# The first token tile multiplied with two weight chunks before the second tile is loaded and transposed

## The reference

```python
h = rmsnorm(x, g_mix[l])        # x: (1, 256, 1024) float32
proj = h @ w_in[l]              # w_in: (1024, 4608) float32
...
x = x + merged @ w_out[l]
h = rmsnorm(x, g_ffn[l])
x = x + jnp.square(jax.nn.relu(h @ w_ff1[l])) @ w_ff2[l]
return rmsnorm(x, g_final)
```

## Time and profile before

| what | value |
|---|---|
| median of three runs | 355.31 us (355.11 to 355.83) |
| the profiled execution, its own time | 355.15 us |
| span of its trace | 353.3 us |
| TensorE busy | 346.1 us (98%) |
| VectorE busy | 253.6 us (72%) |
| ScalarE busy | 186.8 us (53%) |
| DMA | 64.24 MB, mean 182 GB/s |

### The profile page before, as it was taken

How to read it: one execution, slowest core, us unless ns; L and a number is a source line. 1 busy time by engine, 2 the same in 40 slices (tenths; PEclk the granted TensorE clock), 3 DMA queues, 4 the chain that set the end, 5 groups by cost and what they waited for, 6 DMA issues and landing times.

```text
span 353.3 us, 4554 instructions
## 1 busy us (share of the span) xinstructions
PE 346.1 (98%) x1717; PEld 285.6 (81%) x1717; DVE 253.6 (72%) x309; ACT 186.8 (53%) x227; POOL 4.0 (1%) x14
## 2 busy tenths in 40 slices
PE   8999999999999999999999999999999999999993
PEld 4788888777778888888888888888888888888882
DVE  2969999999899889956756737638376383663734
ACT  4995644688885457443654436424364253542413
POOL 1000000000000000000000000000000000000000
PEclk9999999999999999999999999999999999999999
DMA  7999456444533366683637571935719447160003
GB/s 271 353 386 380 169 177 196 160 124 163 181 131 119 121 237 189 231 280 107 206 120 239 181 253 51 334 133 166 255 56 318 155 153 255 67 237 0 0 0 120
DMA packets 34286, 64.24 MB, mean 182 GB/s; under 512 B 1344, under 2 KB 5600, under 8 KB 34272
## 3 DMA queue, kind: packets, MB, share of 16 engines
q1 hardware_dynamic: 33968, 63.52, 53.3%
q10 hardware_dynamic: 304, 0.53, 0.4%
HBM read 63.00 MB, written 1.05 MB: 181 GB/s over the span
## 4 chain that ended last, share of the span: by engine, by line
PE 94%; issue 2%; DMA 1%; SPq 1%; DVE 1%; ACT 1%; POOLq 0%; POOL 0%; DVEq 0%
PE ps L885 20%; PE ps L887 20%; PE ps L886 20%; PE ps L1115 17%; PE ps L1117 9%; PE ps L872 3%; PE ps L931 2%; PE ps L942 1%; DMA raw<-in_w_in_dram 1%; PE ps L985 1%; PE ps L1010 1%; SPq L310 0%; DVE w_lo L630 0%; SPq L314 0%; DVE res L852 0%
## 5 line engine op out<-in xcount | busy, mean ns | idle before, releaser
L885 PE MATMUL ps<-w_hi,a_lo 128*128 128x512 f32 x272 | 107.5, 395 | 0.0
L887 PE MATMUL ps<-w_lo,a_hi 128*128 128x512 f32 x272 | 106.1, 390 | 0.0
L886 PE MATMUL ps<-w_hi,a_hi 128*128 128x512 f32 x272 | 106.0, 390 | 0.0
L1115 PE MATMUL ps<-b_both,w_hi 128*128 128x512 f32 x256 | 90.8, 399 | 0.0
L1117 PE MATMUL ps<-b_both,w_lo 128*128 128x256 f32 x256 | 71.9, 281 | 0.0
L836 DVE TENSOR_TENSOR w_lo<-raw,w_hi 128x2048 fp32r<-128x2048 f32 x28 | 63.5, 2288 | 6.4 <-ACT w_hi L596 6.4
L392 ACT CAST w_hi<-raw 128x2048 fp32r<-128x2048 f32 (+1 forms) x30 | 53.7, 1796 | 18.0 <-PE ps L887 16.8
L622 DVE TENSOR_TENSOR w_lo<-raw,w_hi 128x2048 fp32r<-128x2048 f32 x26 | 59.4, 2288 | 3.4 <-ACT w_hi L392 3.3
L885 PEld LDWEIGHTS ps<-w_hi,a_lo 128*128 128x128 f32 x272 | 51.1, 188 | 11.1 <-issue 0.7
L887 PEld LDWEIGHTS ps<-w_lo,a_hi 128*128 128x128 f32 x272 | 51.0, 188 | 11.0
L886 PEld LDWEIGHTS ps<-w_hi,a_hi 128*128 128x128 f32 x272 | 51.1, 188 | 10.1
(11 more groups left out here) (116 smaller groups left out, 245.1 us busy)
## 6 DMA issues: line engine op xcount, KB each, us to landing
raw<-in_w_ff_dram SPq DMA_DIRECT2D x32, 1024.0 KB, 5.5
raw<-in_w_in_dram SPq DMA_DIRECT2D x14, 1024.0 KB, 5.9
raw<-in_w_out_dram SPq DMA_DIRECT2D x4, 1024.0 KB, 4.9
raw<-in_w_in_dram SPq DMA_DIRECT2D x14, 256.0 KB, 5.1
raw<-in_w_attn_up_dram SPq DMA_DIRECT2D x2, 1024.0 KB, 5.0
raw<-in_w_conv_pw_dram SPq DMA_DIRECT2D x2, 1024.0 KB, 5.0
res<-in_x_dram SPq DMA_DIRECT2D x2, 512.0 KB, 3.9
raw<-in_w_in_dram SPq DMA_DIRECT2D x4, 128.0 KB, 3.9
```

Of the source, the lines that this page charges most:

```text
L885: nc.tensor.matmul(dst, lo[:, tok], w_hi[:, slot, k], start=start, stop=False, skip_group_check=seeded)
L886: nc.tensor.matmul(dst, hi[:, tok], w_hi[:, slot, k], start=False, stop=False, skip_group_check=seeded)
L887: return nc.tensor.matmul(dst, hi[:, tok], w_lo[:, slot, k], start=False, stop=stop, skip_group_check=seeded)
L1115: nc.tensor.matmul(ps[:, TB + c], w_hi[:, slot, k, cols], b_both[:, kk].rearrange("p a t -> p (a t)"), start=kk == 0, stop=False)
```

## The change

x tile 1 is loaded behind chunks 0 and 1 of the weights. PE transposes tile 0 and goes on to the products of tile 0 with chunks 0 and 1; only then does it transpose tile 1, and the products of tile 1 with the two chunks follow. ACT and DVE make `a_hi` and `a_lo` of chunks 0 and 1 for each tile apart (128x128), and DVE makes `w_lo` of chunks 0 and 1 in two instructions of 128x512. The matmuls on zeros ahead of the products go from three to one. The number of matmuls that count, and everything from chunk 2 on, stay as they were.

```diff
-WARM_AGAIN = 3
+WARM_AGAIN = 1
...
-            for t in range(TT):
-                sp.dma_start(res[:, t], x_v[:, t]).then_inc(x_full[t], 16)
+            sp.dma_start(res[:, 0], x_v[:, 0]).then_inc(x_full[0], 16)
             for k in range(2):
                 load_halves(0, slice(k, k + 1), first_full[k])
+            sp.dma_start(res[:, 1], x_v[:, 1]).then_inc(x_full[1], 16)
...
+            act.wait_ge(x0_tr, 1)
+            for k in range(2):
+                nc.scalar.activation(a_hi[:, k, 0:P], x_chunk(k)[:, 0:P], ACT.Copy, scale=gmix[:, k:k + 1]).then_inc(x0_hi, 1)
+            act.wait_ge(first_full[1], 32)
+            nc.scalar.copy(w_hi[:, 0, 1], raw[:, 0, 1]).then_inc(first_hi[1], 1)
             for pair in range(4):
                 act.wait_ge(x_tr, pair + 1)
+                tok = slice(P, T) if pair == 0 else slice(0, T)
                 for k in (2 * pair, 2 * pair + 1):
-                    nc.scalar.activation(a_hi[:, k], x_chunk(k), ACT.Copy, scale=gmix[:, k:k + 1]).then_inc(xt_hi, 1)
-                if pair == 0:
-                    act.wait_ge(first_full[1], 32)
-                    nc.scalar.copy(w_hi[:, 0, 1], raw[:, 0, 1]).then_inc(first_hi[1], 1)
+                    nc.scalar.activation(a_hi[:, k, tok], x_chunk(k)[:, tok], ACT.Copy, scale=gmix[:, k:k + 1]).then_inc(xt_hi, 1)
...
+            for k in range(2):
+                dve.wait_ge(x0_hi, k + 1)
+                input_low(k, slice(0, P), x0_lo)
+            for k in range(2):
+                dve.wait_ge(first_hi[k], 1)
+                nc.vector.tensor_tensor(w_lo[:, 0, k], raw[:, 0, k], w_hi[:, 0, k].bitcast(F32),
+                                        ALU.subtract).then_inc(first_lo, 1)
...
+            for k in range(2):
+                pe.wait_ge(x0_hi, k + 1)
+                pe.wait_ge(first_hi[k], 1)
+                chunk_product(0, k, a_hi, w_hi, start=k == 0)
+                pe.wait_ge(x0_lo, k + 1)
+                chunk_product(0, k, a_lo, w_hi)
+            pe.wait_ge(first_lo, 1)
+            chunk_product(0, 0, a_hi, w_lo)
+            pe.wait_ge(x_full[1], 16)
+            for k in range(KD):
+                last = transpose(x_chunk(k)[:, P:T], res[:, 1, k * P:k * P + P])
+                if k % 2 == 1:
+                    last.then_inc(x_tr, 1)
+            pe.wait_ge(first_lo, 2)
+            chunk_product(0, 1, a_hi, w_lo)
+            for k in range(2):
                 pe.wait_ge(xt_hi, k + 1)
-                pe.wait_ge(first_hi[k], 1)
-                half_products(0, k, a_hi, start=k == 0)
+                chunk_product(1, k, a_hi, w_hi, start=k == 0)
+                chunk_product(1, k, a_hi, w_lo)
+            for k in range(2):
                 pe.wait_ge(xt_lo, k + 1)
-                half_products(0, k, a_lo)
+                chunk_product(1, k, a_lo, w_hi)
```

More of the change, by code:

```diff
@@ L227, in build @@
         vec_made = sem("vec_made")
+        x0_tr = sem("x0_tr")
+        x0_hi = sem("x0_hi")
+        x0_lo = sem("x0_lo")
         x_tr = sem("x_tr")
@@ L635, in _, with input_low @@
             dve.wait_ge(gmix_made, 1)
+            def input_low(k, tok, made):
+                nc.vector.scalar_tensor_tensor(out=a_lo[:, k, tok], in0=x_chunk(k)[:, tok], scalar=gmix[:, k:k + 1],
+                                               in1=a_hi[:, k, tok].bitcast(F32), op0=ALU.mult,
+                                               op1=ALU.subtract).then_inc(made, 1)
+            for k in range(2):
[5 more added lines that the diff above has]
+                                        ALU.subtract).then_inc(first_lo, 1)
             for pair in range(4):
@@ L638, in _ @@
                     dve.wait_ge(xt_hi, k + 1 if pair == 0 else 2 * pair + 2)
[L639 to L645, removed]
+                    input_low(k, slice(P, T) if pair == 0 else slice(0, T), xt_lo)
                 if pair == 1:
@@ L916, in _ @@
             transpose(ps[:, SB0, 0:KD], gmix_rows).then_inc(gmix_tr, 1)
[L917 to L922, removed]
+            pe.wait_ge(x_full[0], 16)
+            for k in range(KD):
+                last = transpose(x_chunk(k)[:, 0:P], res[:, 0, k * P:k * P + P])
+                if k == 1:
+                    last.then_inc(x0_tr, 1)
             for _ in range(WARM_AGAIN):
                 nc.tensor.matmul(ps[:, 0], zero_b[:, 0:P], zero_b[:], start=True, stop=True)
-            def half_products(n, k, a, start=False):
-                for t in range(TT):
-                    nc.tensor.matmul(ps[:, t], a[:, HK * n + k, t * P:t * P + P], w_hi[:, n, k], start=start, stop=False)
             def high_products(n, k):
-                half_products(n, k, a_lo)
-                half_products(n, k, a_hi)
+                for a in (a_lo, a_hi):
+                    for t in range(TT):
+                        nc.tensor.matmul(ps[:, t], a[:, HK * n + k, t * P:t * P + P], w_hi[:, n, k], start=False, stop=False)
             def low_products(n, k):
@@ L944, in low_products, with chunk_product @@
                 return last
-            for k in (0, 1):
+            def chunk_product(t, k, a, w, start=False):
+                nc.tensor.matmul(ps[:, t], a[:, k, t * P:t * P + P], w[:, 0, k], start=start, stop=False)
+            for k in range(2):
[7 more added lines that the diff above has]
+            pe.wait_ge(x_full[1], 16)
+            for k in range(KD):
+                last = transpose(x_chunk(k)[:, P:T], res[:, 1, k * P:k * P + P])
[4 more added lines that the diff above has]
+            for k in range(2):
                 pe.wait_ge(xt_hi, k + 1)
-                pe.wait_ge(first_hi[k], 1)
-                half_products(0, k, a_hi, start=k == 0)
+                chunk_product(1, k, a_hi, w_hi, start=k == 0)
+                chunk_product(1, k, a_hi, w_lo)
+            for k in range(2):
                 pe.wait_ge(xt_lo, k + 1)
-                half_products(0, k, a_lo)
-            pe.wait_ge(first_lo, 1)
-            for k in (0, 1):
-                low_products(0, k)
+                chunk_product(1, k, a_lo, w_hi)
             pe.wait_ge(xt_lo, 4)
```

## The result

The changed kernel takes 356.23 us (median of 10 runs, 355.66 to 356.69) against 355.24 (10 runs, 355.02 to 355.83): a ratio of 1.0024, 95% interval 1.0017 to 1.0032. It is slower by 0.99 us in the medians, just beyond the 0.2% (0.7 us) up to which I had called a change told from none. The profiled execution has 356.50 us and a span of 354.7, for 355.15 and 353.3 before.

What follows compares the result with a forecast made beforehand. TensorE bounds the kernel, so the head counts only through the start of chunk 2's first product. ScalarE's later `high(0)` moves that by +0.17 us: 355.31 + 0.17, about 355.5 us; range 354.9 to 356.5.

Steps and rivals of the forecast that it cites:

- S: Start of chunk 2's first product on TensorE: 10.18 us before, forecast at 10.35, with everything behind it moving along.
- no change that can be told: Whole kernel: time within 0.2%, 0.7 us, of the kernel before; chance 0.75.
- my own sign: Start of chunk 2 on TensorE: the sum is wrong if it comes before 10.0 or after 10.8 us.
- the slow cases: TensorE's clock staying low, 356.1 to 357.0 us, chance 0.12; x tile 1 landing later than 7.7, chance 0.10.
- two waits ending together at 10.12: Ahead of chunk 2's first product: one wait the change shortens, another set by the DMA of chunks 2 and 3.
- The landings: Early loads: chunk 0 at 5.09, chunk 1 at 5.78, x tile 1 at 7.12, chunks 2 and 3 still at 8.96.
- My upper bound, 7.6: Latest landing of x tile 1 in the forecast, from the largest latency of 4.3 us; S would move +0.4.
- Tile 0: First tile's transposes and products: ScalarE's first `a_hi` at 4.98, TensorE ready for tile 1's transposes at 7.37.
- The chain from the transposes to S: Tile 1: transposes at 7.37, ScalarE's `a_hi` from 7.85, `high(0)` at 9.13, chunk 2's first product at 10.35.
- x tile 1 late: Rival at tile 1's transposes: landing at 8.4 puts S at +1.2, 356.5 us; chance 0.10 for later than 7.7.
- The clock rival: TensorE's clock stays low after a sparse stretch: S at +0.8 to +1.7, say 356.5 us; chance 0.12.
- The gain: Rival at the head: `high(0)` early enough for chunk 2 to start at 9.82, time 354.95, 0.1% faster; chance 0.08.

Runs made afterwards that it cites:

- tile 0 twice: The changed kernel with the transposes of tile 1 reading x tile 0 again, not waiting for x tile 1: 356.24 us, ratio 1.0023.
- a chunk in one DMA: The changed kernel with chunk 0 and chunk 1 each loaded by one DMA of 256 KB, not two of 128 KB: 356.87 us, ratio 1.0047.
- the late tile without the six matmuls: The kernel before with only x tile 1 issued behind chunks 0 and 1: 359.70 us, ratio 1.0130.
- the busy late tile: The kernel before with x tile 1 issued behind chunks 0 and 1, and six more matmuls on zeros between both tiles' transposes: 357.98 us, ratio 1.0068.

## Why the prediction was right or wrong

The time lay in my range, near its upper end, and the likeliest forecast was not what happened: I had S at 10.35 and 355.5 us, and gave 0.75 to no change that can be told; the kernel is slower by 0.24%. By my own sign the sum was wrong: it was to fail if chunk 2 started after 10.8, and it started at 11.50. The range held only because half of the slow cases had been taken into it.

**What bounds it: right.** The prediction has the head's one moment S and everything behind it moving with it. S moved by 1.32 and the last matmul by 1.32. It has two waits ending together at 10.12, one of which the change doesn't shorten: with the wait for x taken away, that second one was the last to end and held S at 11.28, and with both shortened S went to 9.82. That they ended together in the first profile was partly chance: with the same order of loads chunks 2 and 3 landed at 8.43 to 8.50 in three other profiles.

**The landings: wrong, and this is the step that failed.** "The same bytes in another order give: chunk 0 at 5.09, chunk 1 at 5.78, x tile 1 at 7.12", and chunks 2 and 3 "land at 8.96 still". Chunk 0 was cast from 5.28 and chunk 1 was there by 6.04, near enough; but x tile 1 landed at 8.54 (8.66 to 8.91 in four other profiles of this order, 7.00 in a fifth) and chunks 2 and 3 at 10.01 (10.07 with tile 0 twice). I had moved the steps between landings about like blocks. For most parts of the load that was right: 12 of the 16 parts of x tile 1 were there by 7.16. What failed is the silent premise that the parts of a load land together in any order of the queue, as they did before (0.5 us from first to last; 2.0 in the changed kernel). The rate was 269 GB/s in the stretch in which before had 340, and the landing of a load that others follow came 0.9 us later than that of the same load with nothing behind it. My upper bound, 7.6, from the largest time from issue to landing of the x loads (4.3), was no bound: it was 5.5 here, though the load was issued at 3.07 and not at 3.3.

**Tile 0: too early.** I had ScalarE's first `a_hi` at 4.98 and TensorE ready for the transposes of tile 1 at 7.37. It was 5.29, and the last product of tile 0 started at 7.35, so 7.58 at the usual distance: the clock was still low in tile 0's transposes and in its first product. The wait for x tile 1 hides these 0.2 us here.

**The chain from the transposes to S: right.** From the first transpose of tile 1 to S I had 7.37 to 10.35, 2.98. It was 8.58 to 11.50, 2.92. The terms: ScalarE 0.48 behind the transposes (0.48), `high(0)` 1.28 behind that (1.23), S 1.22 behind that (1.21). The `a_hi` of 128x128, which I had bounded by another instruction's rows, took 1.35 for the four in a row where I had 1.38. One sum in this part was off: 9.23 and 0.87 make 10.10 for the end of VectorE's `a_lo`, and not 10.2; nothing hangs on it.

**The rivals.** What happened is the second one, x tile 1 late, which I had given 0.10 with a price of +1.2 and 356.5 for a landing at 8.4. Measured: 8.54, +1.32, 356.50 in the profile, 356.23 in the median. Its mechanism was incomplete: the run with tile 0 twice shows that chunks 2 and 3 are late as well and hold S nearly as far back, so that the late tile is worth only 0.2 us by itself. The clock rival did not occur as priced in the changed kernel's profile: the clock was low in tile 0's transposes, 0.21 apart, as it was in the second profile of the kernel before, and the first two products were 0.42 apart, the next 0.24. It did occur in part in two variants of it, with tile 0 twice and with a chunk in one DMA (0.79 and 0.71 apart), and put the transposes at 8.10 and 7.97; how many of the changed kernel's ten runs it slowed is not shown. That an idle TensorE loses the clock is real here, though, and was shown: after 2.44 us of idling the granted clock was 0.52, and six matmuls on zeros gave back 1.7 us. The changed kernel idled for only 0.8 us. The Trainium skill's rule (TensorE: Matmul & The Clock Gate, What's actually happening), throttled by default and released by sustained activity, agrees with these rows.

**The gain: right that there is none to have.** I had 0.4 us of the head as the most. The run with S 0.36 earlier had its last matmul 0.05 earlier, because of something that I had not seen: a wait of TensorE for ScalarE's softmax, which the first profile doesn't have and three others do, with an early head and with late ones.

**What stays open.** Why one or two of the sixteen parts stay behind (more in the late tile without the six matmuls), and why the DMA engines move fewer bytes and are partly idle with loads issued, when a load with rows of 4 KB comes behind the four small ones. With the later loads held back the last part is 0.35 behind the fifteenth (7.27, 7.62) where it is 1.0 and more with tile 0 twice and with the busy late tile, which speaks for engines that get out of step, some still on x tile 1 and some ahead of it; the traces do not say which engine made which part. One profile with fewer, larger loads of the chunks ran at the full rate with the parts of x tile 1 together, but was that kernel's fastest run.

## What to carry to other kernels

When a load is moved in a queue, don't carry its landing over from the sum of bytes. The sum told here when most parts of the load had landed, but a wait ends with the last of them, and they can spread by 2 us. Take the spread of times from issue to landing of anything queued in that stretch, and expect the loads behind to move too. Where two waits end within 0.1 us of each other, shortening one is worth nothing, and splitting work so that it starts earlier only makes the other wait visible. An early start of a busy engine is worth no more than the next wait of the others allows; and as one profile of a kernel can lack a wait that its next one has, take a second profile before pricing a gain of some tenths of a microsecond.

## What the runs showed of the hardware that I had not expected

- A load of 512 KB took 3.2 to 3.5 us from issue to landing when first, 4.2 to 4.3 when second, 5.5 to 5.8 behind four small ones, and 4.55 there when nothing followed it (one profile).
- x tile 1 on ScalarE's queue did not add rate: 355 GB/s in the same stretch, and chunk 1 landed 5.06 us after its issue instead of 3.8.
- The rise of TensorE's clock fell ahead of the transposes at 4.44 in one profile of the kernel before and during them in another, with the same instructions; S differed by 0.06 us only. In the first TensorE had waited for halves that the other engines make (0.48 us for `w_lo`), in the second it had no wait and was itself the last.
